# Two products of the first up item moved ahead of the last tile's norm, and the gated values handed over by 512 tokens

## The reference, cut to what matters

```
def rms_norm(x, w):
    y = x * lax.rsqrt(jnp.mean(x * x, axis=-1, keepdims=True) + EPS)
    return y * w

def hybrid_layer(x, ...):
    ...
    mix = jnp.concatenate([hm, ha, hs], axis=-1) @ w_out
    x = x + rms_norm(mix, norm_w[1])
    h = rms_norm(x, norm_w[2])
    ff = (jax.nn.silu(h @ w_gate) * (h @ w_up)) @ w_down
    return x + rms_norm(ff, norm_w[3])
```

## Time and profile before

| what | value |
|---|---|
| median of 3 runs | 2874.38 us (2869.85 to 2876.58) |
| the profiled execution's own time | 2872.21 us |
| its span, first to last instruction | 2870.4 us |
| PE busy | 2736.7 us, 95% |
| DVE, ACT, POOL busy | 63%, 39%, 43% |
| mean granted TensorE clock | 0.975 |
| bytes moved | 199.30 MB, mean 69 GB/s |

### The profile page before, as it was taken

How to read it: one execution, slowest core, us unless ns; L and a number is a source line. 1 busy time by engine, 2 the same in 40 slices (tenths; PEclk the granted TensorE clock), 3 DMA queues, 4 the chain that set the end, 5 groups by cost and what they waited for, 6 DMA issues and landing times. The chain is left out here.

```text
span 2870.4 us, 36030 instructions
## 1 busy us (share of the span) xinstructions
PE 2736.7 (95%) x12868; PEld 2171.8 (76%) x12868; DVE 1809.1 (63%) x2886; ACT 1117.7 (39%) x2094; POOL 1233.2 (43%) x776
## 2 busy tenths in 40 slices
PE   7999999999799999999889999998997999999997
PEld 5677877778588888888766788777785888888885
DVE  4479854583765556665555799546747555666556
ACT  4326434573432223232343274336644222323223
POOL 1238410341555445665433283104326544565545
PEclk9999999899899999999999999999998999999998
DMA  4112310523111111111321133105221111111113
GB/s 132 44 27 84 118 52 25 153 75 117 44 45 60 59 44 44 58 45 63 120 93 30 30 96 111 61 8 178 92 81 51 59 45 45 44 58 58 58 44 125
DMA packets 186881, 199.30 MB, mean 69 GB/s; under 512 B 19312, under 2 KB 162800, under 8 KB 186496
## 3 DMA queue, kind: packets, MB, share of 16 engines
q1 hardware_dynamic: 180992, 176.63, 19.7%
q10 hardware_dynamic: 5760, 20.97, 1.9%
HBM read 158.78 MB, written 38.80 MB: 69 GB/s over the span
## 5 line engine op out<-in xcount | busy, mean ns | idle before, releaser
L2177 POOL TENSOR_TENSOR ring_lo<-ring_sum,ring_hi 128x512 fp32r<-128x512 f32 x212 | 320.5, 1527 | 508.8 <-ACT ring_hi L2258 508.8
L2394 PE MATMUL ps<-form_hi,ring_hi 128*128 128x512 f32 x1232 | 491.6, 399 | 25.8 <-issue 14.5
L2394 PE MATMUL ps<-form_hi,ring_lo 128*128 128x512 f32 x1232 | 489.4, 397 | 0.0
L2394 PE MATMUL ps<-form_lo,ring_hi 128*128 128x512 f32 x1232 | 489.0, 397 | 0.0
L900 PE MATMUL ps<-act_hi,whi 128*128 128x512 f32 x960 | 395.8, 412 | 15.0 <-ACT smr L440 10.9
L2505 DVE TENSOR_TENSOR yacc<-yacc,ps 128x1024 f32<-128x1024 f32 x176 | 214.8, 1220 | 265.0 <-PE ps L2419 265.0
L2258 ACT ACTIVATE ring_hi<-ring_sum 128x512 fp32r<-128x512 f32 x212 | 132.6, 632 | 639.8 <-DVE ring_sum L2462 639.8
L900 PE MATMUL ps<-act_hi,wlo 128*128 128x512 f32 x960 | 379.3, 395 | 0.0
L900 PE MATMUL ps<-act_lo,whi 128*128 128x512 f32 x960 | 378.8, 395 | 0.0
L1315 DVE TENSOR_SCALAR_CACHE_REDUCE ties<-score,kth 128x384 uint8<-128x384 f32 (+5 forms) x396 | 348.5, 943 | 4.8
L603 POOL TENSOR_TENSOR wlo<-raw,whi 128x1024 fp32r<-128x1024 f32 x56 | 137.1, 2448 | 406.2 <-ACT whi L645 406.2
(11 more groups left out here) (323 smaller groups left out, 4725.2 us busy)
## 6 DMA issues: line engine op xcount, KB each, us to landing
raw<-in_w_in SPq DMA_DIRECT2D x56, 512.0 KB, 3.8
ff_raw<-in_w_gate SPq DMA_DIRECT2D x22, 1024.0 KB, 5.4
ff_raw<-in_w_up SPq DMA_DIRECT2D x22, 1024.0 KB, 5.4
ff_raw<-in_w_down SPq DMA_DIRECT2D x22, 1024.0 KB, 5.1
proj_scratch<-stage ACTq DMA_DIRECT2D x40, 512.0 KB, 2.7
wc<-proj_scratch SPq DMA_DIRECT2D x14, 1280.0 KB, 6.7
xmid_scratch<-xres SPq DMA_DIRECT2D x16, 512.0 KB, 2.6
resid<-xmid_scratch SPq DMA_DIRECT2D x16, 512.0 KB, 6.5
```

Source lines behind the costliest of these rows:

```text
L2177: pool.tensor_tensor(flat_form(ring_lo[slot]), src, flat_form(ring_hi[slot]).bitcast(F32), ALU.subtract)\
L2394: mm = pe.matmul(ps[:, PRODUCT_BANK[i], :], w[:, k], a[:, k], start=(k == 0 and m == 0), stop=(k == 3 and m == 2))
```

## The change

It does this, in the order of the program:

- **Layout.** The small tiles (`ident`, `small`, `dskip`, `wnorm`, `bcol`, `below`, `unit_b`, `minus_b`) move from the bottom of SBUF to the top, above `ff_raw[0]`, and `NROW`, `CHUNKS`, `TAIL` and `KEEP` are set so that the large tiles start at multiples of 512 bytes. Before, everything above the 1760 bytes of small tiles was off by them.
- **Opening.** Products 0 and 1 of up 0 are called with banks 4 and 5 and stand on PE before and behind the turn of tile 7; products 2 to 6 of gate 0 and then 2 to 6 of up 0 follow. The first 14 weight forms come in the order of the table `OPENING`, so that the form of gate product 4 is f = 6 and no longer f = 4, and is made in the part of the queues behind all token forms.
- **One remainder.** The EARLIER part of token form 3's remainder moves from POOL to DVE. DVE makes two weight sums behind tile 6 in place of three. ACT takes the first product of gate 0 out before token forms 5 and 6, and DVE the second one between their sums.
- **Gated values.** `down` waits for pieces 0 and 1 before tile 0 and for pieces 2 and 3 before tile 4.
- **First units.** The hi and lo of layer 1's first two weight units move to steps 4 and 5 on ACT and behind tiles 2 and 3 on POOL.
- **Loads.** The load of gate 1's weights waits for 9 weight forms in place of 7; block 0 is written out ahead of SP's loop.

```diff
-        NROW = CONST + 10784
+        NROW = CONST + 11 * KB
...
-        CHUNKS = MIX + 8 * KB + 2496
+        CHUNKS = MIX + 8 * KB + 2560
...
-        TAIL = CHUNKS + 101536
+        TAIL = CHUNKS + 101888
...
-        KEEP = top[0]
+        KEEP = CHUNKS + 81408
...
+        ABOVE = DOWN0 + 8 * KB
+        ident = at(ABOVE, "ident", [P, P])
+        small = at(ABOVE + 512, "small", [P, 96])
...
+            TOKENS_READY = {2: 3, 3: 4, 4: 6, 5: 7, 6: 8}
...
+            OPENING = ((0, 0), (0, 1), (1, 0), (1, 1), (0, 2), (0, 3), (0, 4), (0, 5), (0, 6), (1, 2), (1, 3), (1, 4), (1, 5), (1, 6))
+            FIRST_SUM = {(0, 1): 1, (1, 1): 2, (0, 2): 3, (0, 3): 4, (0, 4): 5, (0, 6): 6}
+            FIRST_DRAIN = {(0, 1): 2, (1, 1): 4, (0, 2): 6, (0, 3): 8, (0, 4): 9, (0, 5): 11, (0, 6): 12}
...
+            product_bank = lambda r, i: 4 + i if early(r, i) else PRODUCT_BANK[i]
...
                 token_hi(act, 3, LAST)
+                first_form_hi(act, 4)
                 act.wait_ge(*t_sum(L, 5))
                 token_hi(act, 4, LAST)
-                first_form_hi(act, 4)
                 first_form_hi(act, 5)
+                act.wait_ge(*x_out[0](L, 16 * NT // 2))
+                first_product(act, gate_t, 0, 0)
                 for i in (5, 6):
...
                     if t == 6:
-                        for i in range(1, 4):
-                            first_sum(v, i)
+                        first_sum(v, 1)
+                        first_sum(v, 3)
...
                 first_sum(v, 4)
-                lo(4, EARLIER, 5)
+                lo(3, EARLIER, 4)
                 v.wait_ge(*d_hi(L, NT))
                 token_sum(v, 2, LAST)
                 token_sum(v, 4, LAST)
                 lo(2, LAST, 6)
                 lo(3, LAST, 7)
+                first_sum(v, 5)
+                lo(4, EARLIER, 5)
                 lo(4, LAST, 8)
                 token_sum(v, 5, EVERY)
+                drain(v, gate_t, 1, 1, 0)
                 token_sum(v, 6, EVERY)
...
-                        load_gate(k + 1, cycle(k), p)
+                    load_gate(k + 1, 9 if isinstance(k, int) and k == 0 else cycle(k), p)
...
-                pool.wait_ge(*t_hi(L, 4))
-                token_lo(pool, 3, EARLIER, t_lo_p)
                 if N < DEPTH:
                     clear_columns(pool)
                 first_form_lo(pool, 4)
                 first_form_lo(pool, 5)
-                form_lo_part(6, 6, 5, (0, 1))
-                pool.wait_ge(*t_lo_v(L, 7))
-                pool.wait_ge(*t_lo_p(L, 3))
+                for f in range(6, 9):
+                    form_lo_part(OPENING[f][1], f, (f + 5) % 6, (0, 1))
+                pool.wait_ge(*t_lo_v(L, 8))
                 for t in range(NT):
                     ins = pool.memset(yacc[t][:, :], 0.0)
...
-                for j in range(6):
-                    form_lo_part(j, 7 + j, j, (1, 1))
+                for f in range(9, 14):
+                    form_lo_part(OPENING[f][1], f, (f + 5) % 6, (1, 1))
...
-                    if N < DEPTH and t in (5, 6):
-                        first_lo(pool, N, t - 5)
+                    if N < DEPTH and t in (2, 3):
+                        first_lo(pool, N, t - 2)
...
-                act.wait_ge(*x_out[0](L, 16 * NT // 2))
-                first_product(gate_t, 0)
-                form_hi_part(6, 6, 5, 0, (0, 1))
-                form_hi_part(0, 7, 0, 1, (1, 1))
-                form_hi_part(1, 8, 1, 1, (1, 1))
+                form_hi_part(4, 6, 5, 0, (0, 1))
+                form_hi_part(5, 7, 0, 0, (0, 1))
+                act.wait_ge(*x_out[1](L, 16 * NT // 2))
+                first_product(act, up_t, 2, 1)
+                form_hi_part(6, 8, 1, 0, (0, 1))
                 gate(0, 0)
...
-                    if N < DEPTH and step in (7, 8):
-                        first_hi(act, N, step - 7)
+                    if N < DEPTH and step in (4, 5):
+                        first_hi(act, N, step - 4)
...
                     pe.wait_ge(*f_lo(L, f + 4))
-                    pe.wait_ge(*h_lo(L, 4 * k + 4))
                     for t in range(NT):
+                        if t % (NT // 2) == 0:
+                            pe.wait_ge(*h_lo(L, 4 * k + 2 + 4 * t // NT))
                         pe.wait_ge(*y_add(L, NT * k + t + 1))
...
                 product(0, 0, 5, 0)
                 product(1, 1, 0, 0)
+                pe.wait_ge(*d_hi(L, NT - 1))
+                product(0, 2, 1, 1)
                 turn_normed(pe, NT - 1)
+                product(1, 3, 2, 1)
                 pe.wait_ge(*d_mix(L, NT))
                 for i in range(2, 7):
-                    pe.wait_ge(*t_lo_v(L, i + 1))
-                    if i == 3:
-                        pe.wait_ge(*t_lo_p(L, 3))
-                    product(i, i, (i + 5) % 6, 0)
+                    pe.wait_ge(*t_lo_v(L, TOKENS_READY[i]))
+                    product(i, i + 2, (i + 7) % 6, 0)
...
-                form_sum_part(6, 6, 5, (0, 1))
-                drain(gate_t, 1, 1, 0)
-                drain(gate_t, 2, 2, 0)
-                form_sum_part(1, 8, 1, (1, 1))
+                form_sum_part(4, 6, 5, (0, 1))
+                drain(v, up_t, 1, 3, 1)
+                form_sum_part(6, 8, 1, (0, 1))
+                drain(v, gate_t, 2, 4, 0)
```

More of the change, by code:

```diff
@@ new lines, in layer @@
+            e_in = [sig(f"e_in{s}", 16 * NT // 2) for s in range(2)]
+            e_end = sig("e_end", 2)
+            last_bank = lambda t: ps[:, 0:2, :].rearrange("p a b -> p (a b)") if t % 2 == 0 else turn_bank(1)
+            STAT_X, STAT_Y = 64, 76
+            N = L + 1
+            cycle = lambda k: 7 + 18 * k
+            up_item = lambda k: 2 * k + 1
+            gate_item = lambda k: 2 * k + 2
+            up_place = lambda i, p: (1, 3 * i + 1) if p == 0 else (0, 3 * i + 3)
+            gate_place = lambda i, p: (0, 3 * i + 2) if p == 0 else (1, 3 * i + 3)
@@ new lines, in drain, with add, copy @@
+            def drain(v, t, i, f, r):
+                src = ps[:, product_bank(r, i), :]
+                def add(quarter, op, after):
+                    q = quarter_of(t, *quarter)
+                    if after:
+                        v.wait_ge(*m_drain(L, FIRST_STEP[after] if opening(r) else 10 * r + after))
+                    v.tensor_tensor(q, q, src, op).then_inc(m_drain.sem, 1)
+                def copy(quarter):
+                    v.tensor_copy(quarter_of(t, *quarter), src).then_inc(m_drain.sem, 1)
+                v.wait_ge(*f_done(L, f + 1))
+                if i == 1:
+                    v.wait_ge(*m_first(L, r + 1))
+                    add((0, 1), ALU.add, 0)
+                    copy((1, 1))
+                if i == 2:
+                    add((0, 0), ALU.add, 0)
+                    add((1, 1), ALU.add, 2)
+                if i == 3:
+                    add((0, 0), ALU.add, 3)
+                    copy((1, 0))
+                if i == 4:
+                    add((0, 0), ALU.add, 5)
+                if i == 5:
+                    add((1, 0), ALU.add, 6)
+                    add((1, 1), ALU.subtract, 4)
+                if i == 6:
+                    add((1, 1), ALU.add, 9)
@@ L1927, in b_scalar @@
                         token_hi(act, 0, EVERY)
-                        for i in range(1, 4):
-                            first_form_hi(act, i)
+                        for f in range(1, 4):
+                            first_form_hi(act, f)
                 token_hi(act, 3, EARLIER)
@@ L2377, in product @@
                     pe.wait_ge(*f_lo(L, f + 1))
-                    later = not (isinstance(r, int) and r == 0)
+                    later = not opening(r) and not early(r, i)
                     if i == 0 and later:
@@ L2427, in turn_of @@
                     f0 = cycle(k)
-                    for i in range(7):
+                    for i in range(2 if isinstance(k, int) and k == 0 else 0, 7):
                         product(i, f0 + i, i % 6, up_item(k))
@@ L2529, in turn_of @@
                     for j in range(1, 7):
[L2530 removed]
+                        drain(v, gate_t, j, f0 + 7 + j, r)
                     form_sum_part(1, f0 + 19, 1, next_place(i, p))
```

200 lines of the change are left out of this document (88 added, 112 removed).

## The result

The changed kernel took 2827.52 us (median of 4 runs, 2826.19 to 2829.66) against 2874.17 us before: ratio 0.984, 95% interval 0.9823 to 0.9857. The direction was right. So, but for the smallest, were the parts that the sum was made of, as the experiments show. The larger half of the gain came from a part that the sum had at nothing: the layout. (The executions of the changed kernel fall into two groups some 12 us apart, by the clock that was granted; these four all lie in the longer one, see the part on the spread.)

What follows compares the result with a forecast made beforehand. PE, busy 95% of the span, was taken as the bound, so gains come from its idle or low-clock time. 6.6 + 5.9 + 0.6 + 5.7 = 18.8 us gave 2855.6 us, own range 2850 to 2862, 2849 to 2865 with the first rival.

Steps and rivals of the forecast that it cites:

- The opening: Start of stage e in each layer: shorter PE waits, 3.3 us gained per layer, 6.6 in both.
- The turn: Tile 7 in the opening of stage e: starts at 737.0 after 1.0 us idle in place of 5.4.
- the 9 us wait: PE stands some 9 us before gate product 4, until 761.4, against 758.77 before.
- up 2: Third product of up 0, in the opening: first matmul at about 773.4, after PE waits 1.7 us; before, 778.44.
- the low stretch behind up 2: Low granted clock after the wait at the third product of up 0: costs 1.6 us, as before.
- The hand sum over one DVE queue: Opening, DVE's instruction durations added from 737.0, plus POOL's holds: the weight sum of gate product 4 ends at 759.5.
- The closes: Start of down 10 in both layers: wait for gated values' lo and low clock go, 5.9 and 5.7 us gained.
- The first units: Border to layer 1: moved remainders let PE's 4.36 us PSUM wait end 0.6 us earlier; bounds -2.3 to 3.5.
- The layout: Tile addresses throughout the kernel: no gain, since matmuls of 512 columns follow each other in 0.23 us at either ring-slot alignment.
- the fourth rival: Slower: new addresses cost matmuls time, 9.5 us per ns on the 233 ns spacing; 2884.0 at 3 ns; chance 0.04.
- signs of being wrong: Product 4 after 764, low clock through 738 to 752, matmul spacing other than 0.233, or residual-load wait before POOL's first add.
- The other three: Opening gives nothing: 2862.2, chance 0.10; gated values don't bind by halves: 2867.2, 0.05; layout shortens transfers: 2854.6, 0.05.

Runs made afterwards that it cites:

- order_only: The changed kernel with the layout of before, all other parts of the change in; 2852.23 us, ratio 0.9931.
- units_back: The changed kernel with hi and lo of layer 1's first two weight units back at steps 7 and 8 and behind tiles 5 and 6; 2822.58 us, one run.
- shift128: The changed kernel with 128 empty bytes under all tiles, so large tiles start at true multiples of 256 bytes; median 2817.34 us.
- layout_only: The kernel before with the layout part of the change alone, every engine's order as before; 2844.24 us, ratio 0.9895.

## Why the prediction was right and where it was wrong

- **The opening**, 6.6 us forecast. `order_only` against before, first product to down 0: 84.39 to 79.86 and 84.42 to 81.82, together 7.1. The turn, the 9 us wait and up 2 came where they were said, within 1.9 us, of which 1.8 is that the stage began that much sooner. The halves of it were uneven, though, 4.5 and 2.6 where 3.3 was said for each: the low stretch behind up 2 came in layer 1 and stayed away in layer 0. That the sum of the two came out is in part luck. The hand sum over one DVE queue, with the time POOL holds the operands added, carried that far.
- **The closes**, 5.9 and 5.7. In `order_only` the stretch with its low clock is 5.8 shorter in both (with the units' 0.6 in the first). Right.
- **The first units**, 0.6. By units_back 2.2 to 2.8: mis-sized, inside its bounds, and not separable from the halves in this close.
- **The layout.** This step failed: "Nothing by the rows: a matmul of 512 columns follows the last in 0.23 us". It had two faults. It read the spacing to 10 ns, where a block of 264 gives it to 0.1 ns and 6 ns make 33 us. And it compared ring slots with each other, one operand, where the pair decides. The second fault is also in the fourth rival's "the spacing is the same over six ring slots": in the block shown above the fourteen products of before ran at 229.7 to 234.1 ns. The trace of before held a sign of the answer. In stage a the token tiles and the weights lay at the same 96 bytes past a multiple of 256, and twelve matmuls there took 2.72 us, 226.7 ns each, where the block shown above has 231.4 and 232.9:

```profile
241.56 0.39 PE L900 MATMUL ps<-act_hi,whi 128*128 128x512 f32 x1
...
244.28 0.39 PE L900 MATMUL ps<-act_hi,whi 128*128 128x512 f32 x1
```

  Two stages with the same instruction, clock and no waits, 6 ns apart, and a change that moves every operand: that should have been a rival with a chance of its own. Of the prediction's signs of being wrong it was "a matmul spacing other than 0.233" that came.
- **The rivals.** The slower one had the mechanism and its price, 9.5 us a nanosecond, and only the sign the other way. With a rival for a faster spacing, priced from stage a at 6.2 ns for products and 4.7 for down, the forecast would have been 2855.6 - 32.8 = 2822.8. The other three did not happen: the opening gave its part, the halves did bind, and the transfers' landing did not change by enough to see (weights 5.4, 5.3 and 5.1 us against 5.4, 5.4 and 5.1), because the new layout has no tile at a multiple of 256 bytes; `shift128`, which has, shows the mechanism.
- **What took back some.** 18.3 + 32.8 = 51.1 would be the sum, and 46.6 came. The layout's part is some 3 us too high in it, as `layout_only` shows. And in the traces stage b of layer 1, up to `mix`, took 6.8 us longer than before (98.34 to 105.15 us), a stretch where `order_only` took 98.4 and `layout_only` 102.3. Before had the long course in layer 0 (105.0) and the short one in layer 1, the changed kernel the long one in both. That is how the clock went in these executions, no cost of the change. The same draw helps `order_only` in layer 0 (102.3), so that its 18.3 is as near to the forecast as it is partly by luck; the parts by themselves are 7.1 + 5.8 + 5.8 = 18.7.

## What to carry to other kernels

Where matmuls run back to back, work out their spacing over some hundred of them in each stage, to a tenth of a nanosecond, and compare stages: a difference at the same clock and size is a cost that no list of waits shows. Let the moving and the stationary operand start at the same place modulo 256 bytes; where the sizes and distances of all tiles are multiples of 256, they all do. And when a change touches addresses, ask what it does to pairs and to their order, not to each tile. (Shown for float32r, 512 columns and a weight load for each matmul; no run tried another form.)

## What the runs showed that was not expected

The spacing of a float32r matmul of 512 columns is 226.7 ns when both operands start alike modulo 256 bytes, about 2 ns more when the moving one starts 64 beyond, and 6 ns more for most other differences, with or without other engines in SBUF. The short spacing sets in only after about seven matmuls; so a chain of 16 showed 4.4 of the 6.1 ns that a chain of 36 showed. Large tiles at true multiples of 256 bytes shortened the landing of 1 MB loads from 5.4 to 5.1 us. And executions of the same kernel fell into two groups 12 us apart, with the difference in stage b, in the opening of stage e and in stage a, by the granted clock.
